# Unread TensorE products and one reordered low half around late attention and the chunked recurrence of a two-layer hybrid encoder

## The reference, cut to what matters

```
h = rmsnorm(x);  projections = h @ w_in
y_a = gated DeltaNet(q, k, v after a short convolution), both directions, chunked: triangular solve, then a recurrence
y_b = differential attention, 4 heads, two softmax maps each
y_c = grouped-query attention, 8 heads of 64, 2 key/value heads
x += (sum_i sigmoid(gate_i) * (y_i @ w_branch_i)) @ w_out
x += hierarchical mixture of experts(rmsnorm(x)): 32 experts, top 1 group, top 2 experts, SwiGLU
```

## Time and profile before

| | |
|---|---|
| three timed executions | 1573.2, 1574.89, 1576.79 us, median 1574.89 |
| profiled execution | 1572.78 us, its span 1570.5 us |
| mean granted TensorE clock | 0.940 |
| TensorE matmul busy | 1288.2 us, 82% |
| VectorE, ScalarE, GpSimd busy | 43%, 28%, 8% |
| mean HBM rate | 313 GB/s |

### The profile page before, as it was taken

One profiled execution on the slowest core, in us unless ns is written; L12 is line 12 of the kernel. 1 busy time (PEld: TensorE's weight loads), 2 busy tenths in 40 slices (PEclk: granted clock), 3 DMA queues, 4 the chain that ended last, 5 costly groups with the idle time before them and its releaser, 6 DMA issues. The chain is left out here.

```text
span 1570.5 us, 42304 instructions
## 1 busy us (share of the span) xinstructions
PE 1288.2 (82%) x17356; PEld 998.3 (64%) x17357; DVE 681.1 (43%) x1682; ACT 445.7 (28%) x902; POOL 121.0 (8%) x110
## 2 busy tenths in 40 slices
PE   7998899998886667668799988999898867666665
PEld 6787687776655455446578876787666645445443
DVE  6667856663221221122286777666522321121222
ACT  4456645551000000000145565554400000000000
POOL 2002630000000000000020044200000000000000
PEclk9999999999998988889899999999999988888988
DMA  9521425599999999999974122446999999999996
GB/s 345 203 78 54 135 103 184 212 387 413 424 426 426 427 428 427 428 427 427 410 258 161 55 83 98 174 166 259 387 385 411 426 427 426 428 428 428 427 427 286
DMA packets 81207, 491.05 MB, mean 313 GB/s; under 512 B 13374, under 2 KB 15958, under 8 KB 53718
## 3 DMA queue, kind: packets, MB, share of 16 engines
q1 hardware_dynamic: 81110, 489.68, 76.9%
HBM read 488.61 MB, written 1.05 MB: 312 GB/s over the span
## 5 line engine op out<-in xcount | busy, mean ns | idle before, releaser
L2111 PE MATMUL ps<-ring,arena 128*32 128x128 f32 x5504 | 207.7, 311 | 122.5 <-DMA ring<-in_expert_w_gate_dram 78.4
L2111 PEld LDWEIGHTS ps<-ring,arena 128*32 128x32 f32 x5504 | 179.0, 125 | 161.9 <-DMA ring<-in_expert_w_gate_dram 80.1
L2210 ACT ACTIVATE arena<-ps 128x128 f32<-128x128 f32 x66 | 18.3, 277 | 498.2 <-PE ps L2111 498.2
L2111 PE MATMUL ps<-arena 128*32 128x128 f32 x2688 | 103.9, 313 | 60.0 <-DMA arena<-in_expert_w_gate_dram 42.7
L2316 DVE COPY arena<-ps 128x256 f32<-128x256 f32 x68 | 28.9, 425 | 276.0 <-PE ps L2077 275.9
L2111 PEld LDWEIGHTS ps<-arena 128*32 128x32 f32 x2688 | 89.2, 127 | 79.9 <-DMA arena<-in_expert_w_gate_dram 49.0
L506 POOL TENSOR_TENSOR small<-small,cst 128x8 f32<-128x8 f32 (+1 forms) x21 | 27.7, 1317 | 1193.4 <-DVE small L782 444.5
L1849 DVE TENSOR_TENSOR w_low<-ring,w_high 128x512 fp32r<-128x512 f32 x126 | 85.8, 706 | 52.0 <-ACT w_high L1773 52.0
L2138 PE MATMUL ps<-ring,arena 128*32 128x256 f32 x1376 | 88.7, 389 | 20.7 <-DMA ring<-in_expert_w_down_dram 19.6
L2375 DVE TENSOR_TENSOR arena<-ps,arena 128x128 f32<-128x128 f32 x66 | 25.0, 379 | 181.5 <-ACT arena L2210 181.5
L2212 ACT ACTIVATE arena<-ps 128x256 f32<-128x256 f32 x66 | 25.3, 383 | 275.3 <-PE ps L2138 275.3
(11 more groups left out here) (375 smaller groups left out, 2416.7 us busy)
## 6 DMA issues: line engine op xcount, KB each, us to landing
ring<-in_expert_w_up_dram SPq DMA_DIRECT2D x42, 2048.0 KB, 40.6
ring<-in_expert_w_gate_dram SPq DMA_DIRECT2D x42, 2048.0 KB, 40.4
ring<-in_w_in_dram SPq DMA_DIRECT2D x28, 2048.0 KB, 8.6
ring<-in_expert_w_down_dram SPq DMA_DIRECT2D x44, 1024.0 KB, 39.4
ring<-in_expert_w_down_dram SPq DMA_DIRECT2D x20, 2048.0 KB, 41.9
arena<-in_expert_w_up_dram SPq DMA_DIRECT2D x20, 2048.0 KB, 41.6
arena<-in_expert_w_gate_dram SPq DMA_DIRECT2D x20, 2048.0 KB, 40.3
arena<-in_expert_w_down_dram SPq DMA_DIRECT2D x20, 2048.0 KB, 42.0
```

What stands on the lines that cost most here:

```text
L2111: ins = pe.matmul(bank_b[32 * g:32 * g + 32, u * P:(u + 1) * P], xg[:, c], spare[u][:, c, g] if from_spare else w[:, u, c, g], start=(c == ...
```

## The change

In late attention, TensorE gets two groups of products that nothing reads. Ahead of the second `turn` of step 4 it waits until the last "tok" piece is out of its bank, and makes two products of 512 columns (identity times `dv`) into `ps[6]` and `ps[7]`. Ahead of the second `turn` of step 6 it waits for the exponentials of step 6, and makes two of 384 columns into `ps[1]`. In the recurrence, GpSimd writes the low half of chunk 4 ahead of the masks and not behind the clearing of `LTO`, and TensorE makes three unread products of 512 columns (identity times half of `QT`) into `ps[1]` and `ps[2]` behind chunk 4. Both layers run it. Nothing that is read is computed otherwise.

```diff
@@ tensor, attention block
                     for m in range(1 if s < 4 else 2):
+                        if (s, m) == (4, 1):
+                            pe.wait_ge(d_empty, fills_at["tok", 1, 1] + 1)
+                            for n in range(2):
+                                pe.matmul(ps[6 + n][:, :], ident, dv[:, n], start=True, stop=True)
+                        if (s, m) == (LATE, 1):
+                            pe.wait_ge(c_exp, LATE + 1)
+                            for n in range(2):
+                                pe.matmul(ps[1][:, 0:384], ident, dv[:, n, 0:384], start=True, stop=True)
                         turn(s, m, first_fill[s] + m)
@@ tensor, recurrence block
                 for q in range(4):
                     dense(q)
+                for n in range(3):
+                    pe.matmul(ps[1 + n % 2][:, :], ident, QT[:, 0:2], start=True, stop=True)
@@ gpsimd, recurrence block
                 pool.memset(XBD, 0.0).then_inc(e_zero, 1)
-                for q in range(3):
+                for q in range(4):
                     early_low(q)
                 for G in range(4):
                     d, t = divmod(G, 2)
                     pool.wait_ge(e_e, G + 1)
                     pool.tensor_tensor(INT[:, G], E[:, G], all_heads(cum[d]), ALU.mult).then_inc(e_m, 1)
                 pool.memset(LTO, 0.0).then_inc(e_zero, 1)
-                early_low(3)
                 pool.memset(DIm, 0.0).then_inc(e_zero, 1)
```

## The result

The changed kernel takes 1564.92 us (median of six runs, 1560.93 to 1566.0) against 1573.59 for the kernel before on the same chip (six runs, 1570.47 to 1576.79): a ratio of 0.9946 with a 95% interval of 0.9923 to 0.9969. That is faster by 8.7 us, 0.54%. The forecast was 1570.9, a gain of 4.0, and its range ended at 1567.6: the sign was right, the size less than half of what came. The profiled execution took 1564.5 us with a span of 1562.3, 8.2 us less than the profiled one of before.

What follows compares the result with a forecast made beforehand. Bound: weight stream in the expert stage, elsewhere the hand-ordered chain, slowed by two clock falls. Profiled 1572.78 - 1.62 (attention) - 2.55 (recurrence) + 0.2 (port) = 1568.8; with the timed median's distance, 1570.9 us, range 1567.6 to 1575.2.

Steps and rivals of the forecast that it cites:

- The bound: Whole kernel: weight stream bounds the expert stage, the hand-ordered chain the other stages; time saved ahead moves the stream forward.
- I pass savings on in full: Expert stages: each microsecond saved before the weight transfers was taken to shorten the whole run by as much.
- The three groups: Unread products in late attention and behind chunk 4: 1.72, 1.29 and 2.58 us, hidden in TensorE's waits, cost 0.
- The stall at 177.41: Layer 1's recurrence: 0.97 us without a releaser behind the clock's return, expected to go with the half clock.
- The port: Recurrence: VectorE blocked by GpSimd's moved work delays the levels; +0.1 us per layer, bounds -0.6 to +0.9.
- The +1.8: Recurrence: cost over two layers if the skill's SBUF contention rule applied to every mask with nothing returned.
- The recurrence, -2.55: Layer 1's recurrence: half clock (1.58 us) and the lone stall (0.97) both go; bounds 0 and -2.55.
- Attention, -1.62: Layer 2's late attention: the half-clock stretch goes, saving 1.62 us; bounds 0 and -1.62.
- Sum against the profiled execution: Whole kernel: 1572.78 - 1.62 - 2.55 + 0.2 = 1568.8 us, from one profiled execution.
- More than forecast: Rival: timed runs fall in all four passages and the change clears them; up to 8.3 us less, halfway 1568; chance 0.10.
- Attention keeps its fall: Rival: transposes and narrow products keep late attention's clock falling, only the recurrence gains; 1572.5 us, chance 0.24.

Runs made afterwards that it cites:

- e4: Only the move of low half 4 ahead of the masks, no unread products, against the kernel before: 1573.5 us, ratio 0.9989.
- f3: The kernel before with 14 products of 2 columns (56 instructions) at the start of layer 1: 1572.22 us, ratio 0.9993.
- h1: The kernel before with 32 products of 2 columns (128 instructions) at the start of layer 1: 1569.71 us, ratio 0.9977.
- g3: The changed kernel with 50 more products of 2 columns, its layer 2 expert stage 256 instructions later than in the kernel before: 1566.18 us, ratio 0.9953.
- h2: The changed kernel measured again, unaltered: 1564.98 us, ratio 0.9943 to the kernel before.
- e3: Only the recurrence's part, the move of low half 4 and the three products behind chunk 4, against the kernel before: 1568.59 us, ratio 0.9966.
- g2: The changed kernel with the first attention group (ahead of step 4's second turn) cut to 2 columns: 1567.61 us, ratio 0.9963 to the kernel before.
- g4: The changed kernel with one more unread product of 384 columns ahead of step 7's first turn: 1563.4 us, ratio 0.9940 to the kernel before.
- h3: The changed kernel with the extra 384-column product ahead of step 7's first turn, measured again: 1562.79 us, ratio 0.9928 to the kernel before.
- e2: Only the two attention groups at full width, no change in the recurrence, against the kernel before: 1565.67 us, ratio 0.9948.
- g1: The changed kernel with the second attention group (ahead of step 6's second turn) cut to 2 columns: 1565.19 us, ratio 0.9947 to the kernel before.

## Why the prediction was right and wrong

*The bound.* "I pass savings on in full": it held as far as can be told. Fitted over the seventeen profiles, the end of the span follows the start of layer 2's expert stage with a slope of 1.1 (standard error 0.2). The end of layer 1's expert stage follows its start with 0.9 (0.14), but the first copy of layer 2's attention only with 0.7 (0.13), so a part of layer 1's savings may be given back. But the sentence let me pass through the expert stage without a term.

*The three groups.* Right in each size: 0.15, 0.25 and 1.06 us left of the gaps, all four passages' turns in time, the spread still last, and no idle time ahead of chunk 4. The stall at 177.41 went too, though hardly through the clock: with 0, 56, 128 or 156 instructions more ahead of it, it is there (e4 1.44 us, f3 0.99, h1 0.88, g3 1.54), with 12 to 32 it is there in one profile of twelve (h2, 0.43). It goes by the place of the code, like the one in the expert stage, and in each of these profiles it ends 1.4 to 1.6 us behind an instruction packet.

*The port.* Right in mechanism, +0.02 where I took +0.1. The rule of the Trainium skill (SBUF — State Buffer, "Who interferes with whom") held: 1.40 us behind mask 4 against 0.43 alone. The +1.8 that it would have made, applied to every mask, did not come.

*The recurrence, -2.55.* Right in the pair of profiles (-2.3); in the mean over a third less (-1.6), part of it the stall just named.

*Attention, -1.62: **this step failed.*** The "Sum against the profiled execution" took one execution's falls for what an execution loses. Its two attention passages lost 0.0 and 1.6; the seven profiles without the groups lose 4.7 on average, between 1.5 and 8.6. The saving was about 3.6 in place of 1.62. Of ten passages of the five kernels whose attention code is that of the kernel before (before, e3, e4, f3, h1), eight fell, and not one in two. I also read the place wrong: the sum gave the whole gain to the second group, since the only fall seen was behind it, and took the first group as harmless, worth nothing; g2 says that without the first the gain of attention does not come. The warning stood in the profile and I used it for one rival only: a gap of 1.87 us ahead of step 4, wider than the one behind which the clock had fallen. "More than forecast" had the mechanism (falls that this execution did not show), and I gave it 0.10; its halfway figure should have been 1568.8, between 1570.9 and 1566.7.

*Attention keeps its fall.* Half true: in four of the six profiles with both groups and the gap of 0.76 us left, one passage of the two still falls (148.6 us above), in transposes and narrow products as that rival said. The Trainium skill (TensorE: Matmul & The Clock Gate, "Part 4: PE-mode transpose") says that a transpose does not count as busy in the same way; from that I had taken that the fall stays whatever is put ahead. The runs do not bear this out: with the 0.76 us filled too, four passages of four (g4, h3) were clean. Four are few: with the gap open four of twelve fell.

*What had no term.* The place of the code: 2.7 to 3.9 us by the estimates above, a third or more of the gain. Of the stalls without a releaser I had weighed one, at 177.41, and as a thing of the clock; 3.58 us of the same kind at 1137.14 stood in the same trace, and I did not ask what 56 more instructions would do to either. That the length moves the stall is shown (e2 has it 32 instructions on, g3 back in its place, h1 has none in the first expert), and that it ends with the arrival of an instruction packet is shown too. That the packet comes late because the weight stream fills DMA is argued. What the stall costs is not settled: e3, only 24 instructions longer, has none in the first expert, e2 has one of 3.53 us and loses little by it, and g1, with the changed kernel's length and none there either, has its rest at 439.1.

## What to carry to other kernels

Where the clock falls in some passages and not in others, one profile is one draw: price a marginal place by how thin it is, over several executions, and fill the widest gap too, whether or not the profile shows a fall behind it. And whatever makes an engine's program longer or shorter moves its stalls without a releaser; before a small gain or loss is put down to an edit, run the kernel with the same number of harmless instructions in a hidden place.

## What the runs showed of the hardware

- Every idle time of TensorE of over 1 us without a releaser (189 in seventeen traces, up to 3.58 us) ended 1.1 to 1.7 us behind the end of a 16 KB packet of the instruction queue. Between two packets TensorE started a median of 243 to 267 records.
- 128 instructions more in an idle time, which touch no other timing, gained 3.7 us of the median (h1, ratio 0.9964 to 0.9990); 56 gained 1.7, inside the noise (f3). 256 more bring the old stall back within one record of its place (3.58 us in the kernel before, 1.72 in e4, 2.20 in g3).
- The clock fell behind gaps under 2 us: at 135.4 us in e3 with TensorE busy for 1.53 of the 3.4 us before, and at 148.6 in the changed kernel with 2.39 of 3.4.
- Kernels with the same code in late attention lost between 0 and 4.6 us per layer there, all of it in passages with a stretch at half clock. The median of the kernel before moved by under 1 us over its five measurements (1573.4 to 1574.3).
